# Third layer's attention scores: three f32r products of high and low parts in place of one f32 product, with the pieces' order moved

## The reference

```python
h = rmsnorm(x, norm_pre)
proj = einsum('bld,de->ble', h, w_in)     # z_ssd, xbc, dt, q, k, v, z_sb, gates
...
def stick_breaking(q, k, v):
    for blk in range(L // 128):
        q0 = blk * 128; kend = q0 + 128
        logits = einsum('bqhd,bkhd->bhqk', q[:, q0:kend], k[:, :kend]) * Dh ** -0.5
        mask = ki < qi
        log_fail = where(mask, log_sigmoid(-logits), 0.0)
        between = cumsum(log_fail, reverse=True) - log_fail
        w = where(mask, exp(log_sigmoid(logits) + between), 0.0)
        outs.append(einsum('bhqk,bkhd->bqhd', w, v[:, :kend]))
...
y_sb = (o * silu(z_sb)) @ w_sb_proj
out = x + rmsnorm((g_ssd * y_ssd + g_sb * y_sb) @ w_out, norm_post)
```

## Time and profile before

| | us |
|---|---|
| median of 3 runs | 1231.12 |
| lowest and highest run | 1229.39, 1233.16 |
| the profiled execution | 1233.21 |
| its span, first to last instruction | 1231.5 |
| TensorE busy in the span | 1201.4 (98%) |
| VectorE, ScalarE, GpSimd busy | 536.0, 593.5, 415.6 |
| the stage with the third layer's scores | 843.9 to 1013.0 |

### The profile page before, as it was taken

One profiled execution on the slowest core, in us unless ns is written; L12 is line 12 of the kernel. 1 busy time (PEld: TensorE's weight loads), 2 busy tenths in 40 slices (PEclk: granted clock), 3 DMA queues, 4 the chain that ended last, 5 costly groups with the idle time before them and its releaser, 6 DMA issues. The chain is left out here.

```text
span 1231.5 us, 16504 instructions
## 1 busy us (share of the span) xinstructions
PE 1201.4 (98%) x6273; PEld 933.0 (76%) x6273; DVE 536.0 (44%) x996; ACT 593.5 (48%) x1247; POOL 415.6 (34%) x235
## 2 busy tenths in 40 slices
PE   8999989999999999999999999999999999999998
PEld 8988845568998666668888976787666667878886
DVE  4202555562410455552566644701776760032333
ACT  6345555554533555563554653534556552333242
POOL 5543401105254222225244323344222224444451
PEclk9999989999999999999999999999999999999999
DMA  8433201203134999813222412234111112323231
GB/s 290 122 105 78 64 18 33 69 18 99 58 120 93 61 94 61 123 52 88 70 86 62 127 52 69 69 88 116 53 53 52 52 52 86 103 86 103 86 103 68
DMA packets 111406, 100.99 MB, mean 82 GB/s; under 512 B 21140, under 2 KB 98272, under 8 KB 111328
## 3 DMA queue, kind: packets, MB, share of 16 engines
q1 hardware_dynamic: 108784, 95.35, 32.9%
q0 software_dynamic: 864, 3.15, 0.7%
q10 hardware_dynamic: 1680, 1.44, 0.4%
HBM read 94.68 MB, written 2.10 MB: 79 GB/s over the span
## 5 line engine op out<-in xcount | busy, mean ns | idle before, releaser
L509 POOL TENSOR_TENSOR w_lo<-w_raw,w_hi 128x1024 fp32r<-128x1024 f32 (+6 forms) x169 | 379.3, 2245 | 759.9 <-ACT w_hi L504 759.9
L504 ACT ACTIVATE w_hi<-w_raw 128x1024 fp32r<-128x1024 f32 (+6 forms) x169 | 167.7, 992 | 255.7 <-PE bank L560 228.4
L560 PE MATMUL bank<-acts_hi,w_hi 128*128 128x512 f32 (+1 forms) x592 | 228.9, 387 | 3.9 <-POOL w_lo L509 2.2
L560 PE MATMUL bank<-acts_lo,w_hi 128*128 128x512 f32 (+1 forms) x592 | 227.1, 384 | 0.0
L560 PE MATMUL bank<-acts_hi,w_lo 128*128 128x512 f32 (+1 forms) x592 | 227.0, 383 | 0.0
L560 PEld LDWEIGHTS bank<-acts_hi,w_hi 128*128 128x128 f32 x592 | 111.2, 188 | 28.7 <-issue 5.1
L560 PEld LDWEIGHTS bank<-acts_lo,w_hi 128*128 128x128 f32 x592 | 111.3, 188 | 22.2
L560 PEld LDWEIGHTS bank<-acts_hi,w_lo 128*128 128x128 f32 x592 | 111.3, 188 | 21.1
L560 PE MATMUL bank<-w_hi,acts_hi 128*128 128x512 f32 (+4 forms) x308 | 109.5, 356 | 4.0 <-POOL w_lo L509 1.7
L560 PE MATMUL bank<-w_hi,acts_lo 128*128 128x512 f32 (+4 forms) x308 | 108.6, 353 | 0.0
L560 PE MATMUL bank<-w_lo,acts_hi 128*128 128x512 f32 (+4 forms) x308 | 108.3, 352 | 0.0
(11 more groups left out here) (275 smaller groups left out, 2044.9 us busy)
## 6 DMA issues: line engine op xcount, KB each, us to landing
w_raw<-in_w_in SPq DMA_DIRECT2D x64, 512.0 KB, 3.6
w_raw<-in_w_out SPq DMA_DIRECT2D x24, 512.0 KB, 3.6
w_raw<-in_w_in_b SPq DMA_DIRECT2D x22, 512.0 KB, 5.2
w_raw<-in_w_in_a SPq DMA_DIRECT2D x10, 512.0 KB, 3.8
w_raw<-in_w_mem_kv SPq DMA_DIRECT2D x8, 512.0 KB, 8.0
w_raw<-in_w_sb_proj SPq DMA_DIRECT2D x8, 512.0 KB, 3.4
w_raw<-in_w_ssd_proj SPq DMA_DIRECT2D x8, 512.0 KB, 3.5
arena_shared<-junk SPq DMA_DIRECT2D x11, 256.0 KB, 20.6
```

The source lines that it names most:

```text
L504: nc.scalar.activation(w_at(p)[0][:, 0:size], w_raw[p % RAW][:, 0:size], ACT.Copy).then_inc(w_high.sem, 1)
L509: nc.gpsimd.tensor_tensor(lo[:, 0:size], w_raw[p % RAW][:, 0:size], hi[:, 0:size].bitcast(F32), ALU.subtract).then_inc(w_rest.sem, 1)
L560: mm = nc.tensor.matmul(bank_of(S, s, g)[0:lhs.shape[1], 0:rhs.shape[1]], lhs, rhs, start=j + kk + t == 0, stop=j == len(S.pieces) - 1 and ...
```

## The change

The scores are no longer one f32 matmul for each head but three f32r ones that add up in the same bank: high q by high k, high q by low k, low q by high k, each for both heads before the next. For these ScalarE copies a piece's product out of PSUM twice, first rounded into `qk_hi`, then as f32 into `qk_raw`, and raises `qk` after the second. GpSimd (new `stick_pool`) subtracts the high from the raw part, in place, and raises the new semaphore `qk_low`; this subtraction stands in its queue ahead of the low part of the piece after next. The first score of a pair waits on `qk_low` instead of `qk`. The raw and low parts lie in `hn`, which is free in this stage; the high ones lie where `s_qT` and `s_kT` lay.

The table of products is changed: 58 stand before step 0 instead of 52, then in steps of four (8, 6), (8, 2), (8, 6), (8, 2) instead of (8, 6), (8, 2), (10, 6), (8, 0) (with four fewer in step 0), and the last steps have fewer. Before, an even piece ended at the end of step 4k + 1 and an odd one in step 4k + 3, ahead of the transposes. Now an even piece ends at the end of step 4k and an odd one at the end of step 4k + 2. In `stick_act` the copy and the split move to these steps, both behind `collect_w`.

The diff:

```diff
--- before.py
+++ after.py
@@ -235,6 +235,8 @@
         w_raw = [sb(f"w_raw{n}", [P, PIECE]) for n in range(RAW)]
         with nc.sbuf_tensor("seg_words", [P, 4 * D], BF16) as seg_words:
             pass
+        with nc.sbuf_tensor("hn_parts", [P, 2 * D], F32R) as hn_parts:
+            pass
         hn = sb("hn", [P, 2, D])
         chosen = sb("chosen", [P, C_H + MB])
         tri_mid = sb("tri_mid", [P, P])
@@ -258,6 +260,8 @@
         pos_i = sb("pos_i", [P, MB], I32)
         pos_f = sb("pos_f", [P, MB])
         done_t = sb("done_t", [P, 1])
+        with nc.sbuf_tensor("arena_parts", [P, AR0], F32R) as arena_parts:
+            pass
         arena = sb("arena", [P, AR0])
         with nc.sbuf_tensor("arena_shared", [P, AR1 - AR0], F32) as arena_shared:
             pass
@@ -1353,7 +1357,7 @@
             "head_turned", "conv_turned", "conv_in", "conv_acc", "conv_out", "xT_turned", "xT_out", "ssd_dt", "ssd_sc", "ssd_sc_out",
             "ssd_seg", "chosen_made", "acs_parted", "parts_turned", "seg_in", "ssd_fall", "ssd_exp", "ssd_att", "ssd_diag", "ssd_y", "ssd_state",
             "ssd_prev", "ssd_off", "ssd_off_out", "ssd_ready", "ssd_gated",
-            "z_silu", "n_in", "n_hi", "n_lo", "z", "qk", "sig", "scan", "scan_one", "w", "turned_w", "wT", "s_out",
+            "z_silu", "qk_low", "n_in", "n_hi", "n_lo", "z", "qk", "sig", "scan", "scan_one", "w", "turned_w", "wT", "s_out",
             "s_y", "y_hi", "y_lo", "merged", "m_hi", "m_lo")}
         started = {}
         sem = {n: c.sem for n, c in misc.items()}
@@ -1738,8 +1742,10 @@
         PAIRS = C_H // 2
         STEPS = 4 * PAIRS
         BLOCKS = (3, 0, 2, 1)
-        s_qT = [cut(14336 + n * 512, T) for n in range(2)]
-        s_kT = [cut(15360 + n * 512, T) for n in range(2)]
+        qk_hi = [[arena_parts[:, 14336 + x * 1024 + n * 512:14336 + x * 1024 + n * 512 + T] for n in range(2)]
+                 for x in range(2)]
+        qk_lo = [[hn_parts[:, x * 1024 + n * 512:x * 1024 + n * 512 + T] for n in range(2)] for x in range(2)]
+        qk_raw = [[hn[:, x, n * 512:n * 512 + T] for n in range(2)] for x in range(2)]
         fail = [cut(16384 + n * 512, T) for n in range(4)]
         win = [cut(at, T) for at in (18432, 18944, 23552, 24064)]
         left = [cut(24576 + n * 516, 516) for n in range(2)]
@@ -1790,13 +1796,15 @@
                     return
                 p, b, _, n = item(2 * s)
                 if s % 4 == 0:
-                    pe.wait_ge(sem["qk"], 2 * p + 2)
+                    pe.wait_ge(sem["qk_low"], 2 * p + 2)
                 if s >= 2:
                     pe.wait_ge(sem["sig"], 4 * s - 4)
-                for e in range(2):
-                    rows = slice(HD * e, HD * e + HD)
-                    nc.tensor.matmul(bank[2 + (2 * s + e) % 4][:, 0:n], s_qT[p % 2][rows, b * P:(b + 1) * P],
-                                     s_kT[p % 2][rows, 0:n], start=True, stop=False)
+                for t in range(3):
+                    q, keys = (qk_hi, qk_hi, qk_lo)[t][0][p % 2], (qk_hi, qk_lo, qk_hi)[t][1][p % 2]
+                    for e in range(2):
+                        rows = slice(HD * e, HD * e + HD)
+                        nc.tensor.matmul(bank[2 + (2 * s + e) % 4][:, 0:n], q[rows, b * P:(b + 1) * P],
+                                         keys[rows, 0:n], start=t == 0, stop=False)
                 for e in range(2):
                     mm = nc.tensor.matmul(bank[2 + (2 * s + e) % 4][:, n - P:n], ident_b[:, :], not_before[:, :],
                                           start=False, stop=True)
@@ -1827,13 +1835,12 @@
                                               wT[e][:, c, c * P:T], start=c == 0, stop=c == MB - 1)
                 mm.then_inc(sem["s_out"], 1)
 
-            turn_in(48 + 4)
+            turn_in(48 + 10)
             for s in range(STEPS + 1):
                 score(s)
-                before, after = ((8, 6), (8, 2), (10, 6), (8, 0))[s % 4]
-                before -= 4 * (s == 0)
-                if s >= STEPS - 4:
-                    before, after = ((6, 6), (6, 6), (6, 6), (6, 0), (6, 0))[s - STEPS + 4]
+                before, after = ((8, 6), (8, 2), (8, 6), (8, 2))[s % 4]
+                if s > STEPS - 4:
+                    before, after = ((6, 2), (6, 2), (4, 0), (4, 0))[s - STEPS + 3]
                 turn_in(before)
                 if s % 4 == 1:
                     values(s // 4 - 1)
@@ -1842,6 +1849,15 @@
                 turn_in(after)
             pe.wait_ge(sem["sig"], 4 * STEPS)
             project_pe(pe, pC_gate, between=lambda s: values(PAIRS - 1) if s == 0 else None)
+
+        def stick_pool(pool):
+            S = pC_qk
+            for q in range(S.n):
+                lo, raw, hi = (part[q % 2][q // 2 % 2] for part in (qk_lo, qk_raw, qk_hi))
+                pool.wait_ge(sem["qk"], q + 1)
+                nc.gpsimd.tensor_tensor(lo, raw, hi.bitcast(F32), ALU.subtract).then_inc(sem["qk_low"], 1)
+                pool.wait_ge(w_high.sem, S.piece0 + q + 3)
+                rest(S.piece0 + q + 2, piece_size(S, 0, q + 2))
 
         def stick_act(act):
             S = pC_qk
@@ -1856,8 +1872,10 @@
                 act.wait_ge(C["product"].sem, S.done_after(0, q, 0))
                 if p >= 2:
                     act.wait_ge(sem["z"], 4 * p - 4)
-                nc.scalar.activation((s_qT, s_kT)[q % 2][p % 2], qk_bank(q)[:, :], ACT.Copy,
-                                     scale=(HD ** -0.5, 1.0)[q % 2]).then_inc(sem["qk"], 1)
+                for part in (qk_hi, qk_raw):
+                    ins = nc.scalar.activation(part[q % 2][p % 2], qk_bank(q)[:, :], ACT.Copy,
+                                               scale=(HD ** -0.5, 1.0)[q % 2])
+                ins.then_inc(sem["qk"], 1)
 
             def split(q):
                 split_ahead_act(act, S, 0, q)
@@ -1895,15 +1913,12 @@
                 p = s // 4
                 chances(2 * s)
                 chances(2 * s + 1)
-                if s % 4 == 3 and s < STEPS - 1 or s == STEPS:
-                    collect(2 * PAIRS + 1 if s == STEPS else 2 * p + 3)
                 collect_w(2 * s - 2)
                 collect_w(2 * s - 1)
-                if s % 4 == 1:
-                    collect(2 * p + 2)
-                    split(2 * p + 2)
-                if s % 4 == 3 and s < STEPS - 1 or s == STEPS:
-                    split(2 * PAIRS + 1 if s == STEPS else 2 * p + 3)
+                if s % 2 == 0 and s < STEPS - 2 or s == STEPS:
+                    q = 2 * PAIRS + 1 if s == STEPS else 2 * p + 2 + s % 4 // 2
+                    collect(q)
+                    split(q)
 
         def stick_dve(dve):
             def weigh(p):
@@ -2081,7 +2096,8 @@
             project_pool(pool, pC_zs)
             pool.wait_ge(sem["ssd_gated"], 2 * MB)
             pool.dma_start(row[:, :], i["norm_post_2"].partition_broadcast(P)).then_inc(row_in.sem, 16)
-            for S in (pC_qk, pC_g0, pC_gate, pC_sb, pC_ssd, pC_out):
+            stick_pool(pool)
+            for S in (pC_g0, pC_gate, pC_sb, pC_ssd, pC_out):
                 project_pool(pool, S)
 
         @block.scalar
```

## The result

| | before | after |
|---|---|---|
| median, lowest and highest run (four each), us | 1231.23 (1229.39 to 1233.16) | 1238.40 (1237.39 to 1240.82) |
| ratio of the times, with its 95% interval | | 1.0061 [1.0041, 1.0080] |
| the profiled execution and its span | 1233.21, 1231.5 | 1240.82, 1239.0 |
| the stage, from its first product to the first of the gates behind it | 169.13 | 175.32 |
| from there to the end | 218.43 | 218.45 |

The change costs 7.2 us of the median; the prediction said 1237.6, +6.5. The interval of the ratio, +5.0 to +9.8 us, lies above the bound of 0.3% (3.7 us). Beside the experiments before was timed again in three sets of 15, 23 and 17 runs, with medians of 1231.2 to 1231.4; one of them, 1330.72 us at a granted clock of 0.851, was in a slower state and counts in no ratio.

The account below looks back on a forecast made before the run. TensorE's queue was taken to bound the stage. Terms of -2.0, +5.0, +3.6, +0.3, +0.5, -0.5 and -0.4 summed to +6.5 us on 1231.12, giving 1237.6 us, range 1231 to 1243.

Parts of the forecast that it names:

- The bank's wait: The next piece's first product waits for the second copy of bank 0: +5.0 and +3.6 us, +0.3 for a gate.
- TensorE goes on 0.05 after its end: Step at the piece's copy: TensorE resumes 0.05 us after the copy ends, so the next piece starts at 1.56 us.
- the two terms: Bank waits after seven even pieces, 7 x (1.56 - 0.85) = +5.0 us, and seven odd ones, 7 x (1.56 - 1.05) = +3.6.
- The scores: Three f32r products a head: 512 keys 0.91 us for 1.06, 384 keys 0.75 for 0.85; -2.0 us over eight pairs.
- no load hidden: Case at the scores: second and third weight loads don't hide behind the product before; scores' sum +0.4 us.
- the 0.02s: Allowance of 0.02 us for each of a score's three products; without them the scores save 3.0 us, not 2.0.
- The third rival: At the scores: the two heads' f32r products don't run side by side; +8 us, 1245.6 us, chance 0.06.
- The first score: At the stage's start, the first score waits for GpSimd's low part, ready at 3.1 us instead of 2.6: +0.5 us.
- What goes: The wait at each pair's first score for the copy goes, -0.5 us; near the end, TensorE's wait for VectorE, -0.4.
- The first rival: At the pieces' ends, copies are done when TensorE arrives, so no waits come; 1228.7 us, chance 0.16.
- The second rival: GpSimd's subtraction and split hold up VectorE, so transposes wait in seven pairs: +4.9 us, 1242.5 us, chance 0.11.
- the scan of the 256-key step would end at about 6.0: Step on VectorE: GpSimd's split holds this scan, last weights come at 7.7 us, TensorE wants them at 7.8.

Follow-up runs that it names:

- e1: The kernel before with only the change's product order and copy and split places, scores and single copy as before: stage 170.49 us, median 1232.68, ratio to before 1.0005.
- e5: The changed kernel, but ScalarE reads the bank once, frees it, then rounds the high part from SBUF: stage 168.69 us, median 1230.93, ratio to before 0.9996.
- e4: The changed kernel with pieces summed in two banks in turn, even ones in bank 1: stage 165.07 us, median 1227.30, ratio to before 0.9960.
- e3: The changed kernel with one f32 matmul a head over the rounded parts, copies and subtraction kept: stage 177.81 us, median 1239.92, ratio to before 1.0067.
- e8: The two-bank kernel e4 with one f32 matmul a head over the rounded parts: stage 167.61 us, median 1229.88, ratio to before 0.9993.
- e10: The two-bank kernel e4 with a second, unread 512-column GpSimd subtraction for each piece: stage 171.54 us, median 1233.66, ratio to before 1.0020.
- e2: The changed kernel with the old order, 52 products ahead of step 0 and old copy places: stage 194.57 us, median 1255.37, ratio to before 1.0190.
- e9: The two-bank kernel e4 with two more products ahead of the stage's first score, 12 for 10: stage 165.12 us, median 1227.30, ratio to before 0.9963.

## Why the prediction was right, point by point

**The bank's wait** was the term that decided, and it held in place and kind: 14 waits for the second ACTIVATE. Its size was 1.66 where I had 1.56. The step "TensorE goes on 0.05 after its end" failed: I read it at the 512-key score, where TensorE's load carries the wait for the copy itself. A piece's first product has two waits, and the one for the copy (line 1785, `qk`) is an instruction of its own in the queue of the loads, ahead of the load. The view of line 1785 in after (PEldq is the sequencer of the loads; number, then shortest, median and longest in ns):

```profile
L1785 PEldq EVENT_SEMAPHORE  x16: 51/51/51, 852.2 to 1008.0; - x16
```

There TensorE goes on 0.14 after the copy's end in after (893.96 + 0.59 = 894.55 to 894.69), in e1 (889.66 to 889.80) and in e5 (891.66 to 891.81, 0.15). How long TensorE had stood doesn't decide it: in e1 it was ready 0.13 us before, and at the 512-key score of before the load had stood 0.27 us and went on after 0.05. That the instruction of 51 ns makes the difference is read from the traces and wasn't tried. 14 x 0.1 = 1.4 us were missing: the two terms are +5.7 and +4.3, not +5.0 and +3.6. e4 confirms them from the other side: each of its first seven pairs takes 1.42 us less than in after, 9.9 of the 10.25, and the stage's end 0.3, the gate's.

**The scores**: 0.89 and 0.73 us for 512 and 384 keys, 0.91 and 0.75 predicted; -2.3 and not -2.0 us over eight pairs. e3 and e8 give 2.5; in e8 the smaller scores are in it. In 128 keys I had 0.47 and the trace 0.48. The second and third load do hide: the three double products start 0.33 and 0.23 us apart and the masks 0.33 behind them, as for products on all rows, which start 0.31 apart behind masks and 0.23 apart else. (The Trainium skill, "TensorE: Matmul & The Clock Gate", Part 3, The mechanism, would put a load between the products of a head, 0.21 us more for a score. It doesn't hold here: the score takes 0.89 us.) What the prediction gave for no load hidden, +0.4, left out the 0.02s that its -2.0 has: with them it is 1.12 and 0.96 us, +1.4 in the sum, 3.4 us more and not 2.4. The third rival falls with the same rows, since the heads' products start together.

**The first score** was late by 0.32 to 0.34 us, 0.5 predicted; GpSimd's step took 1.29 to 1.32 us in 15 of 16 cases, within the 1.2 to 1.5, and 0.15 less than the 1.45 of the sum.

**What goes** was undersized. I had -0.5 for eight pairs; e1 shows -0.15 a pair, -1.2 in eight. I don't know how it divides between the load's wait and the transposes that no longer stand at the piece's end. A term was missing besides, -0.6 in the first pair, which I hadn't read row by row. The stage's end came out near the sum, -0.46, where the gate (+0.3), the last pair's scores (-0.25) and the wait for VectorE (-0.4) make -0.35, but not by my reason: the wait for VectorE didn't go, it shrank from 0.43 to 0.29 us (in e1, without a subtraction, to 0.20). These two, what goes and the first pair's term, made up for the 1.4 us too little at the bank, so +6.5 against the measured +6.2 is closer than its terms are: that much is luck.

**The first rival**, no waits, is refuted: e4 shows what that kernel would be. I had put it at 1228.7, and with two banks it is 1227.3.

**The second rival**, GpSimd against VectorE, had its mechanism right and the cover wrong. I had 0.1 us and it was 0.8. The step that failed is "the scan of the 256-key step would end at about 6.0": in after this scan starts at 895.80, 0.07 ahead of the split, and ends after 0.69, so that the product and not the scan is held, and the last weights are there 7.04 us after the odd piece's last product (900.08 - 893.04) instead of 7.7; TensorE wants them at 7.93 (7.8 predicted). GpSimd pays too: its split takes 2.80 instead of 2.40. (That an engine that comes second is held until the first is through, whichever it is, is what the Trainium skill states in "SBUF — State Buffer", section "SBUF: two separate sides". The trace agrees in kind: the split, begun under the scan, takes 0.40 more than alone, and the product, begun under the split, ends at 898.96, 0.29 after the split's end at 898.67.) e10 gives the price once a doubled step has used the cover up.

## What to carry to other kernels

Before an accumulator is copied twice, ask who waits for its bank: here 0.5 us more of ScalarE's time a piece, which ScalarE had to spare, cost 6.6 us of TensorE's, and the wait for the bank 10 in all, four times what the cheaper matmuls gave. A second bank, with two waits on finished work, turned +0.6% into -0.4%. When a wait goes, the room that it gave to others goes with it (VectorE's 0.8 us became 0.2): try the next bound (e10) before a gain is promised on top.

## What the runs showed of the hardware that I had not expected

TensorE's clock can fall inside a stage that is otherwise dense: in e2, soon after six of eight stands of 1.6 to 1.95 us, the granted clock was 0.50 for 3.41 us, at 1.55 us each. What tells these six from the other two isn't known. Two stands of 0.5 to 0.6 us a pair had no such effect in after. What lies between wasn't tried.

TensorE goes on 0.14 us after the end of the ACTIVATE that it waits for, in three kernels, where that wait is an instruction of its own (51 ns) ahead of the load, and 0.05 us where the load itself carries it.

A collision of GpSimd and VectorE is paid by both, and which instruction pays most turns on 0.1 us: a VectorE product of 0.43 took 2.38, a scan of 0.68 took 2.88, a split of 2.40 took 2.80. In e4 GpSimd's subtraction began 0.21 us behind a VectorE product, which took 0.69; in e9 it began 0.12 ahead of it, the product took 1.73, and the gain was gone.
